# Group 0's output projection by seven block products, and the combined weights formed earlier, in four places

## What is computed

```python
u, v, z = jnp.split(h @ w_in, 3, axis=-1)        # h: 2048 x 1024, w_in: 1024 x 6144
u = jax.nn.gelu(u)
v = layer_norm(jax.nn.gelu(v), ln_g, ln_b)
mixed = jnp.einsum("gts,bnsgc->bntgc", ws, vc) + b_s.T[:, :, None]
y = u * mixed.reshape(B, S, A_WIDTH) * jax.nn.silu(z)
return y @ w_out                                  # w_out: 2048 x 1024: the output projection
```

## Time and profile before

| | |
|---|---|
| median of three executions | 2257.64 us |
| profiled execution, whole | 2252.45 us |
| its span, first to last instruction | 2250.7 us |
| TensorE busy | 2175.6 us, 97% |
| TensorE weight loads (beside matmuls) | 1820.2 us |
| VectorE busy | 1428.2 us, 63% |
| ScalarE busy | 1023.9 us, 45% |
| GpSimd busy | 1039.0 us, 46% |
| DMA | 582.35 MB, mean 259 GB/s |

### The profile page before, as it was taken

One profiled execution on the slowest core, in us unless ns is written; L12 is line 12 of the kernel. 1 busy time (PEld: TensorE's weight loads), 2 busy tenths in 40 slices (PEclk: granted clock), 3 DMA queues, 4 the chain that ended last, 5 costly groups with the idle time before them and its releaser, 6 DMA issues.

```text
span 2250.7 us, 28746 instructions
## 1 busy us (share of the span) xinstructions
PE 2175.6 (97%) x10438; PEld 1820.2 (81%) x10438; DVE 1428.2 (63%) x1801; ACT 1023.9 (45%) x1892; POOL 1039.0 (46%) x636
## 2 busy tenths in 40 slices
PE   4999999999999999999999999998999999999998
PEld 4778877888888778888788888887888888887886
DVE  5858864336866864564974653866676667656754
ACT  4334454544454734445644445434444444434542
POOL 3446875555663775544684454440222232232222
PEclk9999999999999999999999999998999999999999
DMA  9677785585888784557876466989676797787654
GB/s 342 238 270 248 271 288 207 191 310 196 314 299 316 277 317 164 197 186 277 312 279 232 167 207 219 356 317 337 232 278 241 264 348 241 266 313 253 217 195 168
DMA packets 242412, 582.35 MB, mean 259 GB/s; under 512 B 20608, under 2 KB 96480, under 8 KB 241888
## 3 DMA queue, kind: packets, MB, share of 16 engines
q1 hardware_dynamic: 239312, 575.22, 70.9%
q10 hardware_dynamic: 2960, 5.30, 0.7%
HBM read 451.47 MB, written 119.54 MB: 254 GB/s over the span
## 4 chain that ended last, share of the span: by engine, by line
PE 74%; DMA 7%; DVE 7%; POOL 3%; ACT 3%; issue 2%; DVEq 2%; POOLq 1%; SPq 1%; ACTq 0%
PE ps L2286 22%; PE ps L2288 21%; PE ps L2287 21%; DMA w_raw<-in_a_w_in 2%; POOL w_lo L1095 2%; PE ps L2489 2%; PE ps L2559 1%; PE ps L2560 1%; PE ps L2585 1%; DVE acc L1731 1%; DMA w_raw<-a_weights_combined 1%; ACT w_hi L1291 1%; DMA b_input<-hbs 1%; PE ps L2594 1%; PE ps L2595 1%
## 5 line engine op out<-in xcount | busy, mean ns | idle before, releaser
L1095 POOL TENSOR_TENSOR w_lo<-w_raw,w_hi 128x1024 fp32r<-128x1024 f32 x244 | 645.0, 2662 | 594.0 <-ACT w_hi L1291 593.4
L1291 ACT ACTIVATE w_hi<-w_raw 128x1024 fp32r<-128x1024 f32 x256 | 268.3, 1058 | 440.3 <-DMA w_raw<-in_a_w_in 349.6
L2286 PE MATMUL ps<-h,w_hi 128*128 128x512 f32 x1024 | 401.9, 392 | 2.7 <-POOL w_lo L1095 1.6
L2288 PE MATMUL ps<-h,w_lo 128*128 128x512 f32 x1024 | 398.8, 389 | 0.0
L2287 PE MATMUL ps<-h,w_hi 128*128 128x512 f32 x1024 | 398.6, 389 | 0.0
L1238 POOL TENSOR_SCALAR_AFFINE_SELECT pt<-pt 128x512 fp32r<-128x512 f32 x128 | 82.2, 642 | 392.7 <-ACT pt L1662 338.1
L2286 PEld LDWEIGHTS ps<-h,w_hi 128*128 128x128 f32 x1024 | 192.2, 188 | 44.5 <-POOL w_lo L1095 3.3
L2288 PEld LDWEIGHTS ps<-h,w_lo 128*128 128x128 f32 x1024 | 192.2, 188 | 40.6
L2287 PEld LDWEIGHTS ps<-h,w_hi 128*128 128x128 f32 x1024 | 192.3, 188 | 39.0
L2286 PE MATMUL ps<-r,w_hi 128*128 128x512 f32 x480 | 191.9, 400 | 0.0
L2288 PE MATMUL ps<-r,w_lo 128*128 128x512 f32 x480 | 187.8, 391 | 0.0
(11 more groups left out here) (274 smaller groups left out, 4798.1 us busy)
## 6 DMA issues: line engine op xcount, KB each, us to landing
w_raw<-in_a_w_in SPq DMA_DIRECT2D x256, 256.0 KB, 3.5
w_hi<-b_weights_split SPq DMA_DIRECT2D x104, 512.0 KB, 4.4
w_lo<-b_weights_split SPq DMA_DIRECT2D x104, 512.0 KB, 5.8
w_raw<-in_a_w_in SPq DMA_DIRECT2D x52, 512.0 KB, 4.7
w_raw<-in_a_w_out SPq DMA_DIRECT2D x52, 512.0 KB, 5.0
w_hi<-v_weights_combined SPq DMA_DIRECT2D x48, 512.0 KB, 3.5
w_lo<-v_weights_combined SPq DMA_DIRECT2D x48, 512.0 KB, 4.7
kv_input<-xks SPq DMA_DIRECT2D x32, 512.0 KB, 7.1
```

The source lines that it names most:

```text
L1095: g.tensor_tensor(wlo[p][:, rows_], raw[p][:, rows_], whi[p][:, rows_].bitcast(F32), ALU.subtract).then_inc(w_lo, 1)
L1291: s_.activation(whi[p][:, rows_], raw[p][:, rows_], ACT.Copy).then_inc(w_hi, 1)
L2286: t_.matmul(dst_, stat[0], mov[0], start=start, stop=False)
L2288: return t_.matmul(dst_, stat[1], mov[0], start=False, stop=stop)
```

## The change

Group 0's output projection takes the form of the other groups: 14 units in seven products, `yb` instead of `y_hl`, and the last sums of the projection go into group 1's v part. For that all "a" combinations must be there before group 0's projection. So all 16 combinations are formed in group 0: two between the v slabs (q = 1), two before the u/z stages (q = 3, as before, but others), and twelve in u/z stages 0 to 6 (q = 4 to 10), two at a time in stages 0 to 3 and 5. They use four places instead of three; the fourth is the half of `y` memory that the second split buffer also uses. Therefore group 0 keeps only two splits, both in the first split buffer, and the later groups have eight each, from q = 3.

```diff
-FIRST = [sum(V_UNITS[:i]) + 16 * i + sum(V_UNITS[:i]) for i in range(NG + 1)]
+OUT_UNITS = 14
+FIRST = [sum(V_UNITS[:i]) + (16 + OUT_UNITS) * i for i in range(NG + 1)]
...
-SPLIT_STAGES = [(i, q) for i in range(NG) for q in range(4 if i else 6, 11)]
+SPLIT_STAGES = [(0, 8), (0, 10)] + [(i, q) for i in range(1, NG) for q in range(3, 11)]
+
+SPLIT_SLOT = [0, 0] + [s % 2 for s in range(2, SPLITS)]
...
-COMBS = [(0, 3, "a", 0, 1), (0, 3, "a", 1, 0)] + [(0, 4 + c, "v", c, (2, 0, 1, 2, 0, 1, 0, 1)[c]) for c in range(8)] \
-    + [(1, 2 + c, "a", c, (0, 2)[c % 2]) for c in range(2, 8)]
+COMBS = [(0, 1, "a", 0, 0), (0, 1, "a", 1, 1), (0, 3, "a", 2, 0), (0, 3, "a", 3, 1), (0, 4, "a", 4, 2), (0, 4, "v", 0, 3),
+         (0, 5, "a", 5, 0), (0, 5, "v", 1, 1), (0, 6, "a", 6, 2), (0, 6, "v", 2, 3), (0, 7, "a", 7, 0), (0, 7, "v", 3, 1),
+         (0, 8, "v", 4, 2), (0, 9, "v", 5, 0), (0, 9, "v", 6, 3), (0, 10, "v", 7, 1)]
...
-        comb_at = (x_at, x1_at, y_at + 16 * K)
+        comb_at = (x_at, x1_at, y_at + 16 * K, y_at)
...
@@ SP, a_stage @@
-                if i == 1 and q == 12:
-                    combs_kept(1)
+                if i == 0 and q == 12:
+
+                    for m in (0, 2):
+                        sp.wait_ge(comb_out[m], combs_out(0, m))
...
@@ SP, the groups @@
+                        if n == 11:
+                            load_split(split_at(i, 3))
...
-                if i == 0:
-                    load_x(1)
-                    for n in range(2, 10):
...
                 for n in range(2, 16):
+                    if i == 0 and n == 15:
+                        combs_kept(0)
                     unit(ao_first(i) + n)
...
@@ POOL @@
                         lo(v_unit(0, 2 * j + 2))
                         lo(v_unit(0, 2 * j + 3))
+                        comb(0, j)
...
@@ ACT @@
+                        if j == 1:
+                            comb(0, 1)
...
                     if m >= 2:
                         act.wait_ge(piece_done, pieces(ao_block(i, m - 2, q), 4))
-                    elif m == 1 and q == 0:
-                        act.wait_ge(comb_out[2], combs_out(i, 2))
+                    elif i == 0 and q == 0:
+                        act.wait_ge(comb_out[3 - m], combs_out(0, 3 - m))
...
@@ DVE @@
-                    late = sv == 0 and i >= 2
+                    late = sv == 0
...
                     v.tensor_tensor(gate_a[:], gate_a[:], ps[:, 3072:4096], ALU.add).then_inc(dve_pro, 1)
+                    comb(0, 1)
                     ada_sum(3)
...
@@ PE @@
-                if i == 0:
-                    project()
-                else:
-                    project_blocks()
+                project_blocks()
```

More of the change, by code:

```diff
@@ L200, in buffers @@
         i = group_of(u) if u < FIRST_B else NG
-        if product_of(u) is not None and (u - FIRST[i]) % 3 == (0 if i == 1 else 2):
+        if product_of(u) is not None and (u - FIRST[i]) % 3 == 2:
             b = 2
@@ L295, in splits_by, with split_before @@
 def splits_by(i, m):
-    return sum(1 for s, (g, _) in enumerate(SPLIT_STAGES) if g <= i and s % 2 == m)
+    return sum(1 for s, (g, _) in enumerate(SPLIT_STAGES) if g <= i and SPLIT_SLOT[s] == m)
+def split_before(s):
+    return SPLIT_SLOT[:s].count(SPLIT_SLOT[s])
 def split_landed(s):
-    return 16 * sum(2 if SPLIT_UNITS[t // 2][0] == "qz" else 1 for t in range(s % 2, s + 1, 2))
+    return 16 * sum(2 if SPLIT_UNITS[t // 2][0] == "qz" else 1 for t in range(s + 1) if SPLIT_SLOT[t] == SPLIT_SLOT[s])
 def split_of(u, hh):
@@ L408, in yoco_kernel @@
         r = place("r", h_at, [KT, 2, T], F32R)
-        y_hl = [place(f"y_hl{s}", y_at + 16 * K * (1 - s), [4, 2, T], F32R) for s in range(2)]
         yb = [place(f"yb{s}", y_at + 16 * K * s, [KT, 2, QT], F32R) for s in range(2)]
@@ L1198, in _ @@
                 comb(i, 3)
+                split(i, 3)
                 for gg in range(GROUPS):
@@ L1502, in _ @@
                         comb(i, 3)
+                        split(i, 3)
                     hi(uz_unit(i, g + 1, 0))
-                    if g == GROUPS - 1 and i == 0:
-                        y_round(0)
-                    elif g == GROUPS - 1:
+                    if g == GROUPS - 1:
                         factor_round(0, 0)
@@ new lines, in _ @@
+                factor_round(0, 1)
+                if i >= 1:
+                    turned_round(i - 1, GROUPS - 1, 7)
+                factor_round(1, 1)
+                factor_round(2, 0)
+                hi(ao_block(i, 1, 1))
+                hi(ao_block(i, 2, 0))
+                out_keep(0)
+                factor_round(2, 1)
+                hi(ao_block(i, 2, 1), (0,))
+                out_keep(1)
+                hi(ao_block(i, 2, 1), (1,))
+                for q in range(2):
+                    factor_round(3, q)
@@ new lines, in _ @@
+                for q in range(2):
+                    hi(ao_block(i, 3, q))
+                for q in range(2):
+                    factor_round(4, q)
+                if i < NG - 1:
+                    x_squares(i + 1)
+                for q in range(2):
+                    factor_round(5, q)
+                if i < NG - 1:
+                    x_scale(i + 1)
+                for q in range(2):
+                    hi(ao_block(i, 5, q))
+                    factor_round(6, q)
+                for q in range(2):
+                    hi(ao_block(i, 6, q))
@@ new lines, in _ @@
+                for c in range(2):
+                    dve.wait_ge(out_kept, out_kepts(i, c + 3))
+                    out_add(i, 1, c, up, up)
+                weights_rest(ao_block(i, 2, 1))
+                factor_rest(3, 0)
+                factor_rest(3, 1)
+                factor_rest(4, 0)
+                dve.wait_ge(tab_out, at("tab_out", i, 16))
+                for c in range(2):
+                    out_add(i, 2, c, up, up)
+                    out_add(i, 2, c, ur, uq)
+                factor_rest(4, 1)
@@ new lines, in _ @@
+                for s in (2, 4):
+                    for q in range(2):
+                        factor_sum(s, q)
+                dve.wait_ge(x1_in, at("x1_in", i, 16))
+                dve.nop(nofuse=True)
+                for c in range(2):
+                    out_done(i, 3, c, uq, 0, c)
+                factor_rest(5, 0)
+                factor_rest(5, 1)
+                factor_rest(6, 0)
+                for c in range(2):
+                    out_add(i, 4, c, ur, ur)
+                    out_add(i, 4, c, uq, uq)
```

273 lines of the change are left out of this document (68 added, 205 removed).

## The result

The changed kernel takes 2262.49 us (median; 2261.19 to 2267.35), 1.0029 times the kernel before, with a 95% interval of 1.0016 to 1.0042. (The ratio compares all executions and not the medians, which lie 4.85 us apart.) That is a little slower, 4 to 9 us, and close to the 0.2% that can be told. The forecast was 2260 us, a little slower than before. Its balance (a shorter projection paid for in the u/z stages) is what the trace shows; two of its terms were off by 4 and 3 us in opposite directions, and smaller ones beside them.

What follows compares the result with a forecast made beforehand. TensorE, busy 97% of 2250.7 us, was taken as the bound. Projection -16.5, later groups -0.4, start +1 and group 0's u/z stages +18.5 gave +2.6 us on the median 2257.64: 2260 us, range 2243 to 2272.

Steps and rivals of the forecast that it cites:

- Projection: Group 0's output projection: 48 matmuls and several waits go, the stretch falls from 100.86 to 84.4 us, -16.5 us.
- rival 4: Group 0's projection misses 84.4 us as yb waits for v4 and v6 to be kept; -10.9, time 2266, chance 0.08.
- Start: Group 0's v part: two added combinations delay ada_sum(3), TensorE waits +1 us, between 0 and +3; ada_sum(4) still early.
- Stage 0: Behind group 0's u/z stage 0: sums beside POOL delay DVE's first wz, stall 2.7 us plus 1.4 at 1.2 GHz.
- Stage 1: Behind group 0's u/z stage 1: wz at 195.2, wanted at 195.4; no stall, but DVE 4 us behind.
- Stage 2: Behind group 0's u/z stage 2: eight table operations and eight sums queue beside POOL; stall 11 us, lower clock +2.5.
- rival 2: Group 0's u/z stage 2: DVE's queue passes before POOL returns, stall 6 us, time 2253, chance 0.18.
- list of signs: Group 0: projection 84 to 85 us, wz wait 10 us or more after 2.8 us sums; wrong if sums run at 0.7.
- Stages 4 to 6: Group 0's u/z stages 4, 5 and 6: losses of 0.9, 0.3 and 0.8 us, plus 1 for late loads.
- Rival 1: Group 0's u/z stages: w_raw halves land 2 to 4 us late, five stages x 2.5 = 12, time 2267, chance 0.22.
- Rival 3: Group 0's u/z stages: unseen POOL gaps or late loads let adds cost 0.7 us, +3 in all, 2245, chance 0.2.
- Groups 1 to 3: Group 1's u/z part loses six combinations, gains one split: -0.4 us; groups 2 and 3: 0, at most +0.5 each.

Runs made afterwards that it cites:

- e1: The changed kernel, with DVE leaving out three of the four additions of combinations a4 to a7 in group 0's u/z stages 0 to 3; 2256.34 us.
- e7: The changed kernel with the second projection unit loaded early and each combination's first two additions put into one 128x1024 DVE instruction; 2256.62 us.
- e9: The changed kernel, with DVE leaving out three of the four additions of a0 and a1 between the v slabs; 2262.48 us.
- e3: The changed kernel, with SP loading group 0's second projection unit before keeping the last combination v7, instead of behind it; 2257.32 us.

## Why the forecast held, point by point

**Projection, -16.5 forecast, -12.48 measured.** The count was right: the rows of the page give three lines of 448 matmuls, 112 each more than the earlier trace rows, so 336 in group 0.

```profile
L2220 PE MATMUL ps<-w_hi,yb 128*128 128x512 f32 x448 | 178.9, 399 | 9.3 <-issue 5.5 <-POOL w_lo L1082 1.9 <-DVE w_lo L1990 1.9
```

The size was wrong by 4 us, and the step that failed is the comparison with group 1. Group 1's projection has no keep in front of its second unit's load; group 0's has, since v7 is formed in stage 6. The prediction counted SP's bytes and asked in rival 4 when the places of v4 and v6 come free, but didn't walk SP's queue past this keep, nor ask that a block unit covers a late load for only half as long. With the load moved the stretch is 84.29: the 84.4 was right for the engines and missed one wait in a queue. Rival 4, `yb` waiting for its places, is refuted by the same figure.

**Start, +1 forecast, +0.48 measured from the first v matmul on, +1.9 to +3.6 in the other kernels.** The v part of the changed kernel is the shortest of thirteen: the others took 106.60 to 108.30 us against 104.72 before. So the term was rather +2 to +3 than +1, at the upper end of the 0 to +3 given, and e1 (+3.58) lies outside it. The wait near 92 is there (0.96 us at 93.11), but not in every kernel with these sums. The statement that `ada_sum(4)` is "still early (112)" was wrong: it ended at 118.5. The step counted DVE's queue alone and left out that POOL's remainders of a0 and a1 now stand beside it, the very effect on which the next part is built.

**Stage 0, stall 2.7 and 1.4 of lower clock forecast.** The stall is 3.07 us on `wz` and 0.87 on POOL before it; the lower level cost 2.0 in place of 1.4. The row, with matmul starts 0.42 apart behind it:

```profile
176.36 0.80 PE L2220 MATMUL ps<-h,w_hi 128*128 128x512 f32 x1 [3.07 <-DVE wz L1946]
```

In all 5.94 us above 23.56, for 4.1 forecast.

**Stage 1, none.** Right: 23.55 us.

**Stage 2, stall 11 and 2.5 of lower clock forecast, 7.56 and 2.5 measured.** The mechanism is the one described. DVE's and POOL's time lines with E1 at 196.96:

```profile
207.28 2.38 DVE L1731 TENSOR_SCALAR tabi<-tabi,freq 128x512 f32<-128x512 int32 x1 [0.17 <-issue]
209.74 2.46 DVE L1734 TENSOR_SCALAR tabs<-tabi 128x512 f32<-128x512 f32 x1
...
220.18 2.69 DVE L1742 SCALAR_TENSOR_TENSOR tabo<-tabs,tabo 128x512 f32<-128x512 f32 x1
222.94 0.69 DVE L1744 SCALAR_TENSOR_TENSOR tabo<-tabs,tabo 128x512 f32<-128x512 f32 x1
223.71 0.43 DVE L1746 TENSOR_SCALAR tabo<-tabo 128x512 f32<-128x512 f32 x1
...
224.56 0.68 DVE L1821 TENSOR_TENSOR cbr<-cbr 128x512 f32<-128x512 f32 x1
...
229.42 2.68 DVE L1826 TENSOR_TENSOR cbr<-cbr 128x512 f32<-128x512 f32 x1
232.03 1.27 DVE L1946 SCALAR_TENSOR_TENSOR wz<-wz,ps 128x512 f32<-128x512 f32 x2
```

```profile
203.63 5.75 POOL L1082 TENSOR_TENSOR w_lo<-w_raw,w_hi 128x1024 fp32r<-128x1024 f32 x2 [6.66 <-ACT w_hi L1274]
209.34 7.67 POOL L1101 TENSOR_TENSOR cbl<-cbr,cbh 128x1024 fp32r<-128x1024 f32 x3
216.97 5.35 POOL L1082 TENSOR_TENSOR w_lo<-w_raw,w_hi 128x1024 fp32r<-128x1024 f32 x2
229.07 5.27 POOL L1082 TENSOR_TENSOR w_lo<-w_raw,w_hi 128x1024 fp32r<-128x1024 f32 x2 [6.75 <-ACT w_hi L1274]
```

The queue starts at E1 + 10.3 (forecast 10.4), six operations pass at 2.4 to 2.7 us beside POOL, and POOL is through at E1 + 25.4 (26.5). The term that was mis-sized is POOL's idle time: forecast 3.7 us, in which four operations pass, measured 6.75, in which all but the last sum pass. It is longer because the load for the `w_hi` that ends it landed late: SP issued it at 220.71, 0.20 behind E2 as in the other stages, and ACT had it only at 227.94, in a stretch with a full queue:

```profile
220.71 0.37 SPq L766 DMA_DIRECT2D w_raw<-in_a_w_in  x1
...
227.94 1.06 ACT L1274 ACTIVATE w_hi<-w_raw 128x1024 fp32r<-128x1024 f32 x1 [6.62 <-DMA w_raw<-in_a_w_in]
...
221.00:228.00 7.00, 4.20 (x26) 3.37 (x24) 6.63 (x10) 0.38 (x2) 1.32 (x1) 0.95 1.03 323
```

So the outcome lies between the forecast and rival 2 (all through, stall 6), next to rival 2, whose time should have read 2254 to 2255 by its own sum (-5 to -6 against 2260). By the prediction's list of signs this is not a clean hit either: it asked for a wait of 10 us or more with sums of 2.8 us before it, and called itself wrong if the sums ran at 0.7. Here the wait is 7.56 us and seven of the eight sums ran at 0.7; what passed at 2.4 to 2.7 and made DVE late were six operations of the table. That DVE operations of two SBUF inputs and POOL's exclude each other is also what the Trainium skill states (SBUF — State Buffer, Who interferes with whom): the trace agrees, 0.69 us alone against 2.7 beside POOL. It states the same of one-input operations such as tensor_scalar when they run in a two-port mode; 0.43 us at 223.71 and 2.46 at 209.74 agree too.

**Stages 4 to 6.** Forecast 0.9 + 0.3 + 0.8 + 1 = 3.0; measured above 23.56: 0.35, 1.09 and 2.17, that is 3.6, and 0.35 in stage 0. Behind stage 5 TensorE waited 0.75 us for `wz`, behind stage 6 0.73 and 0.70 for `w_lo`, the second after ACT had waited 9.30 us for the load of that unit. So late loads are in the largest of the three.

**Rivals.** Rival 1, loads decide: not in stages 0 to 2 (their waits don't answer to more bytes), but from stage 3 on more bytes cost time, and once DVE is relieved of the table late loads are behind up to half of what is left. Rival 3, gaps of POOL: its price is refuted (2245; the waits on `wz` alone are 11.4 us), and the sums ran at 2.7 us wherever POOL worked; but behind E2 there is a gap of POOL that is 3 us longer than forecast, and by it the stall came out 3.4 us under the forecast.

**Groups 1 to 3, -0.4 forecast, -2.7 measured.** Group 1's u/z part went from 190.62 to 190.05 us, which is the forecast term. Of the rest -1.3 is group 3's projection (84.03 to 82.71), which the change doesn't touch and which lay between 82.6 and 84.0 in the other kernels; what is left is within such differences.

So the sum of +2.6 had two failed terms, 4.0 us too much gain in the projection and 3.4 us too much loss behind stage 2. Behind stage 0 it had 1.8 us too little, behind stages 3 to 6 and in stage 0 itself 1.0 too little. These four leave +3.4; that the profiled executions come out within 0.6 us of the forecast (3.15 for 2.6) is due to the start (-0.5) and to groups 1 to 3 (-2.3), mostly differences that the change didn't make. Between the medians it is 4.85 us for 2.6. The sign was earned by the mechanisms, the closeness by luck.

## What to carry to other kernels

When a step is costed by the same step elsewhere, walk every in-order queue past its start in the new place: here a load behind a keep cost 4 us of a gain of 16. When two engines exclude each other, their times add, and moving or merging operations inside the full stretch gave next to nothing here; what helped was to take them out to a stretch with room (17 operations out of group 0 into groups whose u/z parts stayed at 190.0 us: -5.7 us; moved within it they made its part less than 1 us shorter). After that ask what comes next, which was in part late loads, before counting further gains.

## What the runs showed of the hardware

The price of a short wait in clock is not fixed. Ten us each behind the first `wz` wait in three kernels, the changed one (wait 3.07), e7 (2.96) and e9 (3.07):

```profile
176.00:186.00 10.00, 9.64 (x36) 7.91 (x37) 9.73 (x7) 7.43 (x9) 8.90 (x4) 0.83 0.73 277
```

```profile
174.44:184.44 10.00, 9.99 (x44) 8.29 (x45) 9.73 (x6) 6.92 (x9) 9.71 (x4) 1.00 0.73 270
```

```profile
180.00:190.00 10.00, 9.82 (x31) 7.81 (x31) 9.73 (x7) 7.00 (x9) 9.45 (x4) 0.68 0.69 264
```

The granted clock of 1.00 is the 2.4 GHz level, and each loss below it is time at 1.2 GHz. The cost beyond the waits themselves ranged from 0.3 us (e7: 26.82 - 23.56 - 2.96) to 3.2 (e3, wait 2.85) and 3.5 (e9: 31.50 - 23.56, less its waits of 3.07 and 1.40). A wait of 3 us thus cost between 3.3 and 6.5, and the 2.75 us that e7 was shorter than e3 behind stage 0 are this and not its fewer operations, as the waits themselves were 2.96 and 2.85. What decides the price isn't shown by these runs.

A DVE operation of 128x1024 beside POOL took 3.3 to 3.4 us against 2.7 to 2.9 for 128x512, and the pair of POOL instructions of which the first ran beside one took 6.16 us for 5.64. Halving the number of operations by doubling their size saves DVE 2 us for every pair and gives part of it back on POOL.
